# A two-layer diffusion step on one core: branch weight blocks loaded and split in another order, row clearing in five transfers, and layer 2's first projection in two token parts

## The reference, cut to what matters

```python
# per layer l of 2; x: 128 prompt tokens and 512 latent tokens, 1024 features
h = modulate(rms_norm(x, norm1_g[l]), sh1, sc1)        # sh, sc, g: from the condition c
z = h @ w_in[l]                                        # 2816 columns, then 3 x 1024 gates
u_f, q_g, k_g, v_g, q_d, k_d, v_d, gates = split(z)    # u_f: 512 columns, Fourier branch
merged = (sigmoid(g_f) * (fourier_mix(u_f) @ w_f)
        + sigmoid(g_g) * (gqa_attention(...) @ w_go)
        + sigmoid(g_d) * (diff_attention(...) @ w_do))
x = x + g1 * (merged @ w_out[l])
h = modulate(rms_norm(x, norm2_g[l]), sh2, sc2)
x = x + g2 * moe(h, ...)     # 16 experts, top 2 of the best group
# after layer 2: final RMS norm; keys and values of the prompt are outputs too
```

## Time and profile before

| What | Value |
|---|---|
| Median of 3 runs | 2130.22 us |
| Profiled execution, its own time | 2130.46 us |
| Its span, mean granted clock of PE | 2128.6 us, 0.962 |
| PE busy | 1936.0 us (91%), 12731 products |
| DVE, ACT, POOL busy | 1116.8, 878.9, 354.8 us |
| `h_rows` clearing | one DMA of 12800 KB |
| `raw` and `pw` loads | 1024 KB and 512 KB each |

### The profile page before, as it was taken

One profiled execution on the slowest core, in us unless ns is written; L12 is line 12 of the kernel. 1 busy time (PEld: TensorE's weight loads), 2 busy tenths in 40 slices (PEclk: granted clock), 3 DMA queues, 4 the chain that ended last, 5 costly groups with the idle time before them and its releaser, 6 DMA issues. The chain is left out here.

```text
span 2128.6 us, 31233 instructions
## 1 busy us (share of the span) xinstructions
PE 1936.0 (91%) x12731; PEld 1633.1 (77%) x12731; DVE 1116.8 (52%) x1742; ACT 878.9 (41%) x1403; POOL 354.8 (17%) x131
## 2 busy tenths in 40 slices
PE   6999899998999979999779998878999998899994
PEld 5889766698999866677468896557999987676772
DVE  5385267641443346777573743664234343577764
ACT  4333355531212325556344334655221223365553
POOL 1223100031223220000131231000212340200003
PEclk9999899999999989999889998999999999899997
DMA  7312378728221149999441121001212121899954
GB/s 272 107 58 64 111 241 260 237 88 306 66 89 50 66 165 368 311 312 315 164 141 40 60 77 36 2 1 40 90 60 90 60 85 60 349 413 383 311 203 168
DMA packets 163858, 336.34 MB, mean 158 GB/s; under 512 B 10371, under 2 KB 121603, under 8 KB 149253
## 3 DMA queue, kind: packets, MB, share of 16 engines
q1 hardware_dynamic: 151488, 299.63, 40.6%
q0 software_dynamic: 5760, 20.97, 2.6%
q10 hardware_dynamic: 6468, 13.74, 1.9%
HBM read 334.58 MB, written 53.74 MB: 182 GB/s over the span
## 5 line engine op out<-in xcount | busy, mean ns | idle before, releaser
L664 POOL TENSOR_TENSOR wlo<-raw,whi 128x2048 fp32r<-128x2048 f32 x50 | 237.5, 4750 | 1052.7 <-ACT whi L685 1052.7
L1784 DVE TENSOR_TENSOR xw_gu_lo<-xw_gu_raw,xw_gu_hi 128x2048 fp32r<-128x2048 f32 x96 | 219.0, 2284 | 47.6 <-ACT xw_gu_hi L1565 29.5
L170 PE MATMUL psum<-h_hi,whi 128*128 128x320 f32 x896 | 206.1, 311 | 18.7 <-DVE h_lo L155 17.7
L170 PE MATMUL psum<-whi,h_hi 128*128 128x256 f32 x720 | 212.4, 295 | 0.0
L170 PE MATMUL psum<-wlo,h_hi 128*128 128x256 f32 x720 | 206.1, 286 | 0.0
L170 PE MATMUL psum<-whi,h_lo 128*128 128x256 f32 x720 | 206.0, 286 | 0.0
L170 PE MATMUL psum<-h_lo,whi 128*128 128x320 f32 x896 | 205.2, 310 | 0.0
L170 PE MATMUL psum<-h_hi,wlo 128*128 128x320 f32 x896 | 205.1, 310 | 0.0
L1934 PE MATMUL psum<-xw_d_raw,act_T 128*128 128x512 f32 x400 | 179.9, 592 | 0.9 <-ACT act_T L1595 0.9
L1565 ACT ACTIVATE xw_gu_hi<-xw_gu_raw 128x2048 fp32r<-128x2048 f32 x96 | 178.1, 1907 | 1.6 <-DMA xw_gu_raw<-w_e_up 1.6
L1027 DVE TENSOR_REDUCE small_stats<-psum 128x1 f32<-128x640 f32 (+1 forms) x160 | 107.3, 712 | 130.4 <-PE psum L1297 71.1
(11 more groups left out here) (299 smaller groups left out, 3683.3 us busy)
## 6 DMA issues: line engine op xcount, KB each, us to landing
xw_d_raw<-w_e_down SPq DMA_DIRECT2D x50, 1024.0 KB, 9.3
xw_gu_raw<-w_e_gate SPq DMA_DIRECT2D x48, 1024.0 KB
xw_gu_raw<-w_e_up SPq DMA_DIRECT2D x48, 1024.0 KB
raw<-w_in SPq DMA_DIRECT2D x46, 1024.0 KB, 5.4
wm_rest<-w_mod SPq DMA_DIRECT2D x40, 1024.0 KB, 5.2
y_rows<-y_sel SPq DMA_DIRECT2D x50, 512.0 KB, 9.6
h_sel<-h_rows SPq DMA_DIRECT2D x48, 512.0 KB, 7.7
h_rows<-c_zero ACTq DMA_DIRECT2D x1, 12800.0 KB, 45.5
```

The source lines that it names most:

```text
L170: mm = pe.matmul(dst, st, mv[q], start=start and n == 0, stop=stop and n == 2)
L664: pool.tensor_tensor(wlo[i % 2][:, :, :], raw[i % 2][:, :, :], whi[i % 2][:, :, :].bitcast(F32), ALU.subtract).then_inc(w_lo, 1)
L1784: dve.tensor_tensor(gu_lo[i % 2][:, n, :, :], gu_raw[i % 2][:, n, :, :], gu_hi[i % 2][:, n, :, :].bitcast(F32), ALU.subtract).then_inc(x_l ...
```

## The change

- `pw` loads: blocks 0 and 1 first, then each block's `raw` load ahead of the `pw` load of the block two on, instead of `pw` and `raw` by turns of one block on.
- `pw_hi` of the next block comes between the two sigmoids of a block, `pw_lo` between its two merges (from block 1 on for `pw_hi`); both stood at the block's end.
- The wait for `d_k` stands behind the branch groups of block 0.
- `h_rows` is cleared by five DMAs of 5 x 128 rows, in blocks 2 to 6.
- In the seam, PE turns tile t before it sums tile t - 2; the sum of tile 4 moves into layer 2's program; norm and projection are done for tiles 0 to 2 (384 columns), then tiles 3 and 4 (256 columns), with `h_lo` made by DVE throughout. `mul1` is computed in the MoE program, and the table of the root is loaded after the square of tile 2. ACT copies part 0 of `u_T` before the small loads.

```diff
@@ SP, branch stage
-                    for n in range(12):
+                    def load_out(n):
                         b, m = divmod(n, 4)
-                        if n == 0:
-                            sp.wait_ge(t_pv, NA)
...
                         if n >= 2:
                             sp.wait_ge(g_pfull, 2 * (n - 1))
                         sp.dma_start(pw[n % 2][:, :, :], w_br[b][:, :, m * WC:(m + 1) * WC]).then_inc(p_ld[n % 2], 16)
...
+                    load_out(0)
+                    if first:
+                        stream(N_WIN + 1)
+                        stream(N_WIN + 2)
+                    load_out(1)
+                    for n in range(12):
                         stream(N_WIN + 3 + n)
+                        if n + 2 < 12:
+                            load_out(n + 2)
@@ ACT, layer 2's first projection
+                    def parts_act():
+                        act.activation(sq_e[(TT - 1) % 2][:, :, :], x_T[:, :, (TT - 1) * P:TOK], ACT.Square).then_inc(n1_sq, 1)
+                        for p in range(2):
+                            for kc in range(KD):
+                                if p == 0 and kc == 3:
+                                    std_act(act, 1, n1_std)
+                                act.wait_ge(n_t, KD * p + kc + 1)
...
+                                        act.activation(h_mix[:, kc % NH, c0:c1], h_mix[:, kc % NH, c0:c1], ACT.Identity,
+                                                       bias=shift1[:, kc, s:s + 1], scale=mul1[:, kc, s:s + 1]).then_inc(n_h, 1)
+                        for g in range(FG):
+                            act.wait_ge(n_u, g + 1)
+                            act.activation(u_T[:, g, 0:TA * P], pair(g)[:, 0, 0:TA * P], ACT.Copy)
@@ ACT, branch stage
+                            if n >= 1 and fc == 0 and n + 1 < 12:
+                                pw_high(n + 1)
...
-                        if n + 1 < 12:
-                            pw_high(n + 1)
+                        if n == 0:
+                            pw_high(1)
...
-                        if first and n == 2:
-                            act.dma_start(h_rows.rearrange("(t p) d -> p t d", p=P),
-                                          a["c_zero"].unsqueeze(1).to_broadcast([P, N_TILES, D])).then_inc(s_rows0, 16)
+                        if first and 2 <= n < 7:
+                            act.dma_start(h_rows.rearrange("(t p) d -> p t d", p=P)[:, 5 * (n - 2):5 * (n - 1), :],
+                                          a["c_zero"].unsqueeze(1).to_broadcast([P, 5, D])).then_inc(s_rows0, 16)
@@ DVE, layer 2's first projection
+                    def part_dve(p):
+                        c0, c1 = parts[p]
+                        for kc in range(KD + 1):
+                            if kc < KD:
...
+                                dve.tensor_tensor(h_mix[:, kc % NH, c0:c1], x_T[:, kc, c0:c1], rstd_mix[:, c0:c1], ALU.mult).then_inc(n_t, 1)
+                            if kc >= 1:
...
+                                dve.tensor_copy(h_hi[:, kc - 1, c0:c1], h_mix[:, (kc - 1) % NH, c0:c1]).then_inc(n_hi, 1)
+                                dve.wait_ge(n_hi, s)
+                                dve.tensor_tensor(h_lo[:, kc - 1, c0:c1], h_mix[:, (kc - 1) % NH, c0:c1],
+                                                  h_hi[:, kc - 1, c0:c1].bitcast(F32), ALU.subtract).then_inc(n_lo, 1)
+                            if p == 0 and kc == 4:
+                                rstd_dve(dve, 1, n1_std)
+                            if p == 0 and kc == 2:
+                                dve.wait_ge(n1_bc, 1)
+                                var_dve(dve, 1, n1_std)
@@ DVE, branch stage
-                        if n + 1 < 12:
-                            pw_low(n + 1)
+                            if fc == 0 and n + 1 < 12:
+                                pw_low(n + 1)
@@ PE
+                    def project_part(p):
+                        c0, c1 = parts[p]
+                        for kc in range(KD):
+                            pe.wait_ge(n_lo, KD * p + kc + 1)
+                            for g in range(FG):
+                                cs = slice(g % 2 * P, (g % 2 + 1) * P)
+                                mm = mm_split(pe, [pair(g)[:, p, 0:c1 - c0]], whi[g // 2][:, kc, cs], wlo[g // 2][:, kc, cs],
+                                              [h_hi[:, kc, c0:c1]], [h_lo[:, kc, c0:c1]], kc == 0, kc == KD - 1)
+                                if kc == KD - 1:
+                                    mm.then_inc(s_full if p else n_u, 1)
...
-                        pe.wait_ge(d_k, DH)
...
                     branch(0)
                     branch(1)
+                    pe.wait_ge(d_k, DH)
...
-                            else:
-                                sum_tile(t - 1)
+                        if not last and t >= 2:
+                            sum_tile(t - 2)
...
-                        sum_tile(TT - 1)
+                        sum_tile(TT - 2)
@@ DVE, end of layer 1's MoE
-                        dve.wait_ge(e_sum, TT)
...
-                        dve.reciprocal(rstd_mix[:, :], var_mix[:, :]).then_inc(e_rstd, 1)
+                        dve.scalar_tensor_tensor(
+                            out=mul1[:, :, :], in0=nxt[:, 8:16, :], scalar=1.0,
+                            in1=gain_T[:, 0:8].unsqueeze(2).to_broadcast([P, KD, 2]), op0=ALU.add, op1=ALU.mult)
+                        dve.wait_ge(e_sum, TA)
+                        var_dve(dve, 0, e_var)
+                        rstd_dve(dve, 0, e_var)
```

More of the change, by code:

```diff
@@ L347, in build @@
         s_full, s_free = sem("psum_full"), sem("psum_free")
-        s_z, s_rope, s_vs, s_va, s_kc, s_cv = (sem(x) for x in (
-            "rows_used", "rope_done", "row_square", "row_sqrt", "k_cache_loaded", "v_cache_loaded"))
+        s_rope, s_vs, s_va, s_kc, s_cv = (sem(x) for x in (
+            "rope_done", "row_square", "row_sqrt", "k_cache_loaded", "v_cache_loaded"))
         s_r, s_fd = sem("rope_step"), sem("u_folds_ready")
@@ L507, in stat, with squares_act, var_dve, std_act @@
         def stat(t):
-            return psum[:, 5, 0:P] if t == 0 else psum[:, 6, (t - 1) * P:t * P]
+            return psum[:, 6, t * P:(t + 1) * P] if t < TA else psum[:, 7, (t - TA) * P:(t - TA + 1) * P]
+        def squares_act(act, t):
+            act.wait_ge(x_step, t + 1)
+            act.activation(sq_e[t % 2][:, :, :], x_T[:, :, t * P:(t + 1) * P], ACT.Square).then_inc(e_sq, 1)
+        def var_dve(dve, part, done):
+            c0, c1 = parts[part]
+            dve.tensor_scalar(var_mix[:, c0:c1], psum[:, 6 + part, 0:c1 - c0], 1.0 / D, EPS, ALU.mult, ALU.add).then_inc(done, 1)
+        def std_act(act, part, done):
+            c0, c1 = parts[part]
+            act.wait_ge(done, 1)
+            act.activation(var_mix[:, c0:c1], var_mix[:, c0:c1], ACT.Sqrt).then_inc(done, 1)
+        def rstd_dve(dve, part, done):
+            c0, c1 = parts[part]
+            dve.wait_ge(done, 2)
+            dve.reciprocal(rstd_mix[:, c0:c1], var_mix[:, c0:c1]).then_inc(done, 1)
         gu_ld = [sem(f"expert_gate_up_loaded{i}") for i in range(2)]
@@ L665, in lo @@
                                            ALU.subtract).then_inc(w_lo, 1)
-                    pool.wait_ge(n_lo, 1)
-                    for kc in range(1, KD):
-                        modulate_pool(pool, h_mix, kc)
+                    if first:
+                        pool.wait_ge(n_lo, 1)
+                        for kc in range(1, KD):
+                            modulate_pool(pool, h_mix, kc)
                     for i in range(2, N_WIN + 2):
@@ L740, in _ @@
                         act.wait_ge(s_full, n + 1)
-                        if u[0] == "u":
+                        if u[0] == "u" and not first:
+                            act.activation(u_T[:, u[1], TA * P:TOK], pair(n)[:, 1, 0:TOK - TA * P], ACT.Copy).then_inc(s_free, 1)
+                        elif u[0] == "u":
                             act.activation(u_T[:, u[1], :].rearrange("p (a b) -> p a b", a=2), pair(n)[:, :, 0:HALF],
@@ L1190, in _ @@
                         turn_mod(1)
-                    pe.wait_ge(m_done, 1)
+                    if first:
+                        pe.wait_ge(m_done, 1)
                     def feature_major(dst, i, fc, mv_hi, mv_lo, waits=None):
@@ L1231, in _ @@
                             project(kc, (3,))
-                    for kc in range(4 if first else 0, KD):
+                    for kc in range(4, KD if first else 4):
                         project(kc, range(FG))
+                    def project_part(p):
[8 more added lines that the diff above has]
+                                    mm.then_inc(s_full if p else n_u, 1)
+                    if not first:
+                        for f in range(KD):
+                            if f == 0:
+                                pe.wait_ge(n1_sq, 1)
```

(23 more changed lines are left out.)

39 lines of the change are left out of this document (26 added, 13 removed).

## The result

The changed kernel takes 2099.57 us, the median of four runs (2097.15 to 2103.35). The kernel before, run beside it, took 2130.99 (2129.68 to 2137.19). The ratio of the means is 0.9849, with a 95% interval of 0.9824 to 0.9873. It was faster, as forecast, and by 4.4 us more than forecast. On the scale of the forecast, which started from 2130.22, that ratio gives 2098.1 us, just under the lower end of 2099. The profiled execution took 2099.29 us, with a span of 2097.5.

A forecast was written before the change was run, and what follows sets the result against it. PE, busy 91% of the span, was taken as the bound, losing time only by idling or running at its lower clock. Gains 10.8 + 6.8 + 1.9 + 6.9 = 26.4 us off 2130.46 gave a forecast of 2104 us, range 2099 to 2111.

The forecast's parts named there:

- The long stall: Layer 1's branch stage, before 521.94 us: PE's wait for late pw and the slow products after it go, gaining 10.8 us.
- Rival C: Branch stage: the clearing did not hold block 4, so the 10.8 us stay, 2115 us; chance 4%.
- Rival D: Branch stage: DMA bounds blocks 3 to 7, each 28.7 us instead of 21.15, total 2142 us; chance 4%.
- The six short waits: Blocks 9 to 11 of both layers' branch stages: waits on pw_lo of 1.13 us each go, gaining 6.8 us.
- the turned tiles: Before each layer's first branch product: the 0.88 us wait for the last turned diff-attention tile goes, gaining 1.9 us in all.
- The seam: Between the two layers: transposes first and norm and projection in two parts start the Fourier products 6.9 us earlier.
- The last add: Seam: residual adds no longer wait for transposes behind sums, so the last add ends 2.0 us earlier.
- The reciprocal: Seam: reciprocal and steps before it need 384 columns, not 640, ending at 1085.2 instead of 1092.51 us.
- From SyncE's first transfer to the first projection product: Seam, start of layer 2: squaring tile 4 takes 1.1 us, its sum at half clock 3.8; 4.9 us forecast.
- The projection: Seam: 96 products of 384 and 96 of 256 columns take 28.2 us, plus 0.7 for a slow start.
- Into the Fourier products: Seam: from the projection's end at 1120.5 us to the first Fourier product at 1120.9; 0.4 us forecast.
- Rival A: Seam: small loads issued late make PE wait 4.4 us for folds, 2108.5 us; chance 20%.

The follow-up runs named there:

- experiment 2: The kernel before with only the clearing of h_rows cut into five transfers: 2120.12 us, ratio 0.9957.
- 3: The changed kernel with the clearing put back into one transfer: 2100.63 us, ratio 0.9863.
- 5: The kernel before with only the pw loads issued one step earlier, ahead of the raw load: 2116.9 us, ratio 0.9946.
- Experiment 6: The kernel before with only the pw splits moved earlier, behind the first sigmoid and first merge: 2120.94 us, ratio 0.9963.
- experiment 11: The kernel before with only transposes ahead of sums of squares at the end of layer 1: 2128.02 us, ratio 0.9985.
- 4: The changed kernel run again, unchanged, for its spread and a second trace: 2098.62 us, ratio 0.9859.
- 8: The changed kernel unchanged, third sample, partner of the kernel with all waits filled: 2098.34 us, ratio 0.9864.
- 10: The changed kernel unchanged, fourth sample, partner of the kernel with only attention starts and seam filled: 2100.98 us, ratio 0.9855.
- 12: The kernel before with its semaphores numbered as in the changed kernel, no other edit: 2132.27 us, ratio 1.0004.
- experiment 1: The changed kernel's seam alone, with branch stage and clearing as before: 2118.29 us, ratio 0.9955.

## Why the prediction was right in its parts, and where it was wrong

*The long stall, 10.8 forecast, 11.0 measured.* The size was right, and so was the account that late weights made it. The account of what had made them late was half of it. I priced the clearing's pieces and named the `raw` load only in passing. Experiments 2, 3 and 5 show that the stall needed both a whole clearing in flight and SyncE's old order, with the `raw` load just ahead of `pw`. With that order the `pw` load took 28.7 us, and with none just ahead 13.3 and 13.4. Experiment 6 keeps the order and the stall, and so excludes the place of the splits. Rival C, that the clearing had no part in it, falls by experiment 2. But in the changed kernel, with its new order, the clearing in five is not needed for the time: 2100.63 without it against 2098.62 beside it, with the same 21.12 us in block 4. The Trainium skill (DMA: Bandwidth & Descriptors, Queues, rings and completion order) states that a DMA engine consumes one queue's descriptors in order; the trace agrees, with 28.7 against 13.4 us. The same section of the Trainium skill has each DMA engine take turns between its queues by packets, from which the prediction drew that only the pauses between the pieces would help. The trace agrees: the loads landed 1.1 to 2.1 us behind their pieces. Rival D did not come: a piece was over 10.8 to 11.7 us after its issue, in a block of 21.1.

*The six short waits, 6.8 and 7.0; the turned tiles, 1.9 and 2.0.* Right by mechanism. Experiment 6 shows the first to belong to the moved splits alone, and 5 that the moved loads leave them.

*The seam, 6.9 and 7.6.* By its steps:

- The last add: 2.0 us earlier was forecast, and it was 2.1 by the first profile and 1.95 in experiment 11.
- The reciprocal: a further 5.3 us forecast, 5.4 measured.
- From SyncE's first transfer to the first projection product: 4.9 forecast, 4.54 measured. The sum of tile 4 ran at a clock of 0.50, as forecast, behind 5.16 us of idle and not 4.6.
- The projection: 28.9 forecast, 28.26 measured. The term of 0.7 for a slow start was not needed in this profile, since the clock was back when its products began. That was luck: from the first projection product to the first Fourier product it took 28.88 us here, and 29.1 to 29.4 in experiments 3, 4, 8 and 10, where the first products were still slow. The 384 columns took 0.174 us.
- Into the Fourier products: 0.4 forecast, 0.63 measured.

*Rival A* (late small loads) did not come. This timeline answers to the earlier trace rows:

```profile
1092.05 0.50 ACT L775 ACTIVATE u_T<-psum 128x384 f32<-128x384 f32 x1
1092.26 0.45 ACTq L728 DMA_DIRECT2D lam_in<-diff_lambda  x1
...
1096.77 0.48 DVE L1028 MEMSET u_middle<- 128x512 f32 x1
1101.05 0.42 DVE L1033 TENSOR_TENSOR u_folded<-u_T 128x255 f32<-128x255 f32 x1 [3.79 <-ACT u_T L788]
```

The last load was issued 23.6 us after the program's start, and I had 27.2. I had put the DMA issues behind the four copies, one after another; they run beside them. The landing took 3.1 us. The margin was 3.8 us and not 0.8, so the 20% that I gave to this rival was too much.

*The step that failed* is the last of the sum, "2130.46 - 26.4", and the lower end of 2099 that I drew around it. It lets the change gain exactly the sum of its parts. It puts the change of all other stretches at nothing, as one profile had them, without a reason; for the 2100 I counted only steps of the seam. The parts gave 27.6 us, 1.2 more than forecast. The other 3.5 of the 31.1 lie in code that no edit touches, 2.9 of them at the two attention starts (41.1 us before, 38.2 after). Over the five profiles of kernels without the seam edit (before, 2, 5, 6 and 12) the unchanged stretches took 1639.2 to 1645.3 us, mean 1642.5. Here these are the span without the seam, without layer 1's branch stage up to block 4 and from block 9, and without that of layer 2. Over the five of the changed kernel's seam and branch stage (after, 3, 4, 8, 10) they took 1634.4 to 1640.3, mean 1638.1. A forecast from one profile of such a kernel needs some 3 us on either side for that alone.

By how much the forecast was low depends on the comparison. The ratio of the first, 0.9849, puts the time at 2098.1 us, outside the range; its partner had one run of 2137.19, and without it the means give 0.9856 and 2099.6. The ratios of the three repeats (4, 8 and 10) put it at 2100.2, 2101.2 and 2099.3, inside the range and 2.8 to 4.7 us under the 2104.

*What stays open.* The two attention starts took 41.1 to 41.5 us together in those first five profiles, 37.1 to 40.4 in the five others and in experiment 1, and 37.96 in experiment 11. Layer 1's code up to its attention is the same in all. The difference is time at the lower clock level: filling the waits takes it away (33.4), and the same eight products behind the same spell took 2.50 us before and 1.35 after. That the slow stretch is shorter in kernels with an edit in the seam is seen and not explained: semaphore numbers are excluded, and the place of the code in memory was not tried. Each figure is of one profiled execution. The attention starts account for 2.3 of the 4.4 us between the two means above; for the rest there is no account.

## What to carry to other kernels

When a weight load is late beside a large transfer, look first at what stands ahead of it in its own queue, and at what its issue waits for; moving it up cost nothing here and was worth as much as cutting the large transfer. When two edits aim at one stall, price each alone, since the second may add nothing. And look at the granted clock of unchanged stretches in more than one execution before drawing the lower end of a range.

## What the runs showed of the hardware that I had not expected

- Beside a clearing of 12.8 MB, a load of 0.5 MB took 13.3 and 13.4 us with no load of its own queue in flight ahead of it, 14.8 with the last 7.4 us of a 1 MB load ahead, and 28.4 to 28.8 right behind a 1 MB load (five kernels).
- PE ran at the 1.2 GHz level between idle spells of only 1.6 to 2.6 us at the attention starts, and stayed at 2.4 GHz when 21 products that nobody reads filled them.
- ACT's DMA issues ran beside its own activations: three were issued between 1090.94 and 1092.55, while the four copies of `u_T` ran.
